# The first blocks of the first attention inside the projections, and two small jobs moved into the attention

## The reference

```
xr, gr, q, k, v = jnp.split(h @ ev_w_in, 5, axis=-1)        # 512 columns each
xr = causal_dwconv(xr, ev_conv_w, ev_conv_b)
hr = rg_lru(xr, ...)            # gates a, u; recurrence h = a * h_prev + u along the tokens
ya = hr * gelu(gr)
q = rms_norm(q per head of 64, ev_qn_g);  k = rms_norm(k per head, ev_kn_g)
yb = stick_breaking(q, k, v)
mix = concatenate([ya, yb]) @ ev_w_out

# stick_breaking, 8 heads, strictly causal mask
z   = q k^T / 8
sp  = where(mask, softplus(z), 0)
rev = reversed cumulative sum of sp over the keys
out = exp(where(mask, z - rev, -inf)) @ v
```

## Time and profile before

| | |
|---|---|
| median of three runs | 3681.15 us |
| the profiled execution | 3685.37 us |
| its span in the trace | 3683.6 us |
| TensorE busy | 3588.1 us (97%) |
| VectorE busy | 1978.4 us (54%) |
| ScalarE busy | 1333.8 us (36%) |
| mean granted TensorE clock | 0.979 of full |
| projections of q and k, attention | about 107 to 163 us, 163 to 250 us |

### The profile page before, as it was taken

How to read it: one execution, slowest core, us unless ns; L and a number is a source line. 1 busy time by engine, 2 the same in 40 slices (tenths; PEclk the granted TensorE clock), 3 DMA queues, 4 the chain that set the end, 5 groups by cost and what they waited for, 6 DMA issues and landing times.

```text
span 3683.6 us, 41651 instructions
## 1 busy us (share of the span) xinstructions
PE 3588.1 (97%) x16738; PEld 2891.5 (78%) x16738; DVE 1978.4 (54%) x3590; ACT 1333.8 (36%) x2316; POOL 31.8 (1%) x40
## 2 busy tenths in 40 slices
PE   7999999999999999998999999999999999989998
PEld 6668888757888888885788888888878888778886
DVE  7766666675756554576774236423643333354233
ACT  4653333453423332334533223323333233343222
POOL 0000000000000000001100000000000000000000
PEclk9999999999999999999999999999999999989999
DMA  7224555303555455521023222222222222112221
GB/s 280 98 103 149 199 194 177 121 35 121 194 194 194 143 194 194 193 102 40 29 72 100 97 97 81 98 97 97 81 90 82 75 84 82 54 61 97 97 97 63
DMA packets 155613, 429.18 MB, mean 117 GB/s; under 512 B 45483, under 2 KB 50667, under 8 KB 155420
## 3 DMA queue, kind: packets, MB, share of 16 engines
q1 hardware_dynamic: 155420, 426.51, 34.2%
HBM read 424.04 MB, written 2.40 MB: 116 GB/s over the span
## 4 chain that ended last, share of the span: by engine, by line
PE 91%; DVE 6%; ACT 2%; issue 1%; DMA 0%; SPq 0%; POOL 0%; ACTq 0%; DVEq 0%; POOLq 0%
PE ps L427 26%; PE ps L429 26%; PE ps L428 26%; PE ps L746 1%; PE ps L726 1%; PE ps L464 1%; PE ps L786 1%; PE ps L824 1%; PE ps L582 1%; PE ps L599 1%; PE ps L811 1%; PE ps L610 1%; PE ps L477 1%; PE ps L734 1%; DVE wlo L1519 0%
## 5 line engine op out<-in xcount | busy, mean ns | idle before, releaser
L427 PE MATMUL ps<-HH,whi 128*128 128x512 f32 x3168 | 1251.8, 395 | 16.7 <-DVE HL L1576 7.1
L429 PE MATMUL ps<-HH,wlo 128*128 128x512 f32 x3168 | 1236.0, 390 | 0.0
L428 PE MATMUL ps<-HL,whi 128*128 128x512 f32 x3168 | 1235.3, 390 | 0.0
L1519 DVE TENSOR_TENSOR wlo<-wraw,whi 128x1024 fp32r<-128x1024 f32 x548 | 670.8, 1225 | 793.4 <-ACT whi L948 793.1
L948 ACT ACTIVATE whi<-wraw 128x1024 fp32r<-128x1024 f32 x548 | 575.4, 1054 | 714.8 <-PE ps L429 705.9
L427 PEld LDWEIGHTS ps<-HH,whi 128*128 128x128 f32 x3168 | 596.4, 188 | 153.7 <-issue 24.0
L428 PEld LDWEIGHTS ps<-HL,whi 128*128 128x128 f32 x3168 | 596.6, 188 | 125.3 <-issue 4.3
L429 PEld LDWEIGHTS ps<-HH,wlo 128*128 128x128 f32 x3168 | 596.0, 188 | 125.9
L1509 DVE CUSTOM_DVE_ANT_0 mraw<-mraw,CB 128x1024 f32<-128x1024 f32 x224 | 273.0, 1219 | 0.6 <-DMA mraw<-mst 0.6
L1710 DVE TENSOR_TENSOR TT<-TT,ps 128x512 f32<-128x512 f32 x116 | 79.7, 687 | 202.0 <-PE ps L429 171.3
L427 PE MATMUL ps<-PHf,whi 128*128 128x512 f32 x352 | 136.9, 389 | 0.0
(11 more groups left out here) (332 smaller groups left out, 3815.3 us busy)
## 6 DMA issues: line engine op xcount, KB each, us to landing
wraw<-wst SPq DMA_DIRECT2D x548, 512.0 KB, 3.3
mraw<-mst SPq DMA_DIRECT2D x224, 512.0 KB, 4.2
MR<-mst SPq DMA_DIRECT2D x16, 512.0 KB, 14.1
X<-xt SPq DMA_DIRECT2D x8, 256.0 KB, 5.8
BB<-bvec SPq DMA_DIRECT2D x8, 256.0 KB, 3.5
TT<-lse SPq DMA_DIRECT2D x16, 128.0 KB, 2.9
out<-X SPq DMA_DIRECT2D x8, 256.0 KB, 2.0
CB<-crow SPq DMA_DIRECT2D x2, 512.0 KB, 4.4
```

The source lines that it names most:

```text
L427: e.matmul(o[key], wh, sh(k), start=k == 0, stop=False)
L428: e.matmul(o[key], wh, sl(k), start=False, stop=False)
L429: ins = e.matmul(o[key], wl, sh(k), start=False, stop=k == nk - 1)
L1519: e.tensor_tensor(wlo[:, b % RAW, :], wraw[:, b % RAW, :], whi[:, b % SPLIT, :].bitcast(F32), ALU.subtract).then_inc(*wlo_made.up(b))
```

## The change

Logits 0 to 5 stand inside projections 5, 6 and 7 (two each), and the running sums of blocks 0 and 1 inside projection 7. Attention begins with the sums of block 2 and step 6. The head norm of projection 7 is issued in step 6, its root on ScalarE in step 6, its scaling on VectorE ahead of step 7. The rings of banks for norms and logits are reordered. The scratch tiles of `logs` are four in turn (2, 0, 3, 4) instead of five; tile 1 is left to the last norm. The scan writes `YA`, which lies where `YL` lies; `lru_high` is issued in steps 8, 11, 14, 17 and `lru_low` in steps 9, 12, 15, 18. The ten `mod_step`s are issued from step 7 on instead of step 4. Functions not shown here are unchanged; `weights_of` moves out of `stick` with its text unchanged.

```
         YL = at("YL", ph + 8192, [P, 4, S], F32R)
+        YA = at("YA", ph + 8192, [P, 4, S])
...
-        st_slot = (2, 3, 4, 2) + (0, 1, 3, 4, 2) * 6
+        st_slot = (2, 3, 4) * 2 + (2, 0, 3, 4) * 7
...
-            ev_norms = Ring(2, 3, 2, 3, 2, 3, 2, 5)
-            zb = Ring(0, 1, 4, 3, 2, 5)
+            ev_norms = Ring(2, 3, 2, 3, 2, 3, 3, 6)
+            zb = Ring(0, 1, 4, 2, 5, 3)
...
# TensorE, even(): heads(i, k)
+                first_heads = ((5, 5), (5, 7), (6, 1), (6, 5), (7, 1), (7, 5))
...
-                    elif (i, k) in ((6, 5), (6, 7), (7, 1), (7, 5)):
-                        logits(2 * (i - 6) + (k > 5 if i == 6 else k > 1))
+                    elif (i, k) in first_heads:
+                        logits(first_heads.index((i, k)))
+                        if i == 7:
+                            later_sums(first_heads.index((i, k)) - 4)
...
# TensorE, stick(); sums(i) is moved out as later_sums(i), text unchanged
-                qk_norm("ev", 7, ev_order[7], ev_norms)
-                for t in range(3, 39):
-                    if 3 < t < 32:
+                later_sums(2)
+                for t in range(6, 39):
+                    if t < 32:
                         logits(t)
+                    if t == 6:
+                        qk_norm("ev", 7, ev_order[7], ev_norms)
                     if t < 35:
-                        sums(t - 3)
+                        later_sums(t - 3)
...
# ScalarE: lru_high reads YA; even()
-                    if i - 1 in lru_steps:
-                        lru_high(lru_steps.index(i - 1))
                     if i in lru_steps:
                         lru_root(lru_steps.index(i))
+                    if i >= 6:
+                        logs(2 * i - 11)
                     if i == 7:
-                        logs(1)
-                        logs(2)
+                        logs(4)
                     if i:
                         qk_rsqrt("ev", i - 1, ev_order[i - 1])
-                        if i == 6:
-                            logs(0)
-                        elif i == 7:
-                            logs(3)
-                    qk_square("ev", i, m, ev_order[i - 2])
+                    if i in (5, 6):
+                        logs(2 * i - 10)
+                    if i < 7:
+                        qk_square("ev", i, m, ev_order[i - 2])
+                    if i == 7:
+                        weights_of(0)
...
# ScalarE: logs(i)
-                if i < 2:
+                if i < 3:
                     lane.wait_ge(v_mix, ("gi", 3))
-                elif i == 2:
-                    lane.wait_ge(v_mix, ("yl", 3))
-                elif i in (4, 5):
-                    lane.wait_ge(v_mix, ("qk", "ev", ev_order[i + 2]))
+                elif i == 7:
+                    lane.wait_ge(v_mix, ("qk", "ev", ev_order[6]))
                 else:
-                    lane.wait_ge(v_mix, ("a1", i - 5 if i > 5 else 0))
+                    lane.wait_ge(v_mix, ("a1", i - 3 if i < 7 else i - 4))
...
# ScalarE: stick()
-                qk_rsqrt("ev", 7, ev_order[7])
-                weights_of(0)
-                for t in range(4, 39):
+                logs(5)
+                weights_of(1)
+                qk_square("ev", 7, ev_order[7], ev_order[5])
+                weights_of(2)
+                for t in range(6, 39):
                     if t < 32:
                         logs(t)
                     if t < 35:
                         weights_of(t - 3)
+                    if t == 6:
+                        qk_rsqrt("ev", 7, ev_order[7])
+                    if t in (8, 11, 14, 17):
+                        lru_high(t // 3 - 2)
...
# VectorE: lru_scan writes YA[:, m, :] instead of T[4] and no longer waits for ("yl", m - 1); lru_low reads YA; even()
-                    if i - 1 in lru_steps:
-                        lru_low(lru_steps.index(i - 1))
...
-                    if i == 7:
-                        softplus(1)
                     if i:
                         ev_norm(i - 1)
-                    if i >= 6:
-                        softplus(2 * i - 12)
+                    if i >= 5:
+                        softplus(2 * i - 10)
+                        softplus(2 * i - 9)
...
# VectorE: stick()
-                softplus(3)
-                ev_norm(7)
-                for t in range(4, 40):
+                for t in range(6, 40):
+                    if t == 7:
+                        ev_norm(7)
                     if t < 32:
                         softplus(t)
-                    if t % 3 == 1 and t < 34:
-                        mod_step(29 + (t - 4) // 3)
+                    if t in (9, 12, 15, 18):
+                        lru_low(t // 3 - 3)
+                    if t % 3 == 1 and t < 36:
+                        mod_step(29 + (t - 7) // 3)
```

More of the change, by code:

```diff
@@ L586, in logits, with later_sums @@
                          stop=True, skip_group_check=True).then_inc(*mm_done.up(("z", h, kt)))
+            def later_sums(i):
+                h, kt = block_of(i)
+                n, o = wid[kt], ps[:, bank_of[("z", h, kt)], :]
+                later, ones = CR["nlater"][:], CR["nones"][:]
+                lane.wait_ge(v_mix, ("spl", i))
+                for k2 in range(kt, 4):
+                    n2 = wid[k2]
+                    for part in (SPH, SPL):
+                        ins = e.matmul(o[:, n - n2:n], later if k2 == kt else ones, part[h % 3][:, off[k2]:off[k2] + n2],
+                                       start=False, stop=k2 == 3 and part is SPL, skip_group_check=True)
+                ins.then_inc(*mm_done.up(("lat", h, kt)))
             def stick():
                 ob = Ring(6, 7)
[L590 to L601, removed]
                 def heads_out(h, kt):
@@ L1135, in lru_high @@
                 lane.wait_ge(v_mix, ("ya", m))
-                e.activation(YH[:, m, :], T[4], ACT.Copy).then_inc(*a_mix.up(("yh", m)))
+                e.activation(YH[:, m, :], YA[:, m, :], ACT.Copy).then_inc(*a_mix.up(("yh", m)))
             def even():
@@ L1200, in logs, with weights_of @@
                 e.activation(l, l, ACT.Ln, bias=1.0).then_inc(*a_mix.up(("log", i)))
-            def stick():
[L1204 to L1211, removed]
-                qk_rsqrt("ev", 7, ev_order[7])
-                weights_of(0)
-                for t in range(4, 39):
+            def weights_of(i):
+                h, kt = block_of(i)
+                n, o = wid[kt], off[kt]
+                lane.wait_ge(mm_done, ("lat", h, kt))
+                if h >= 3:
+                    lane.wait_ge(mm_done, ("so", h - 3))
+                e.activation(SNB[h % 3][:, o:o + n], bank(("z", h, kt))[:, 0:n], ACT.Exp).then_inc(*a_mix.up(("w", h, kt)))
+                freed[("z", h, kt)] = ((a_mix, ("w", h, kt)),)
+            def stick():
+                logs(5)
[3 more added lines that the diff above has]
+                for t in range(6, 39):
                     if t < 32:
@@ L1813, in lru_scan @@
             def lru_scan(m):
-                z, xc = T[4], XC[:, m, :]
+                z, xc = YA[:, m, :], XC[:, m, :]
                 lane.wait_ge(a_mix, ("sqr", m))
@@ L1818, in lru_scan @@
                 lane.wait_ge(a_mix, ("lb", m))
-                if m:
-                    lane.wait_ge(v_mix, ("yl", m - 1))
                 e.tensor_tensor_scan(z, RR[:, m, :], xc, 0.0, ALU.mult, ALU.add).then_inc(*v_mix.up(("scan", m)))
@@ L1825, in lru_low @@
             def lru_low(m):
-                keep_low(YL[:, m, :], T[4], YH[:, m, :], a_mix, ("yh", m), ("yl", m))
+                keep_low(YL[:, m, :], YA[:, m, :], YH[:, m, :], a_mix, ("yh", m), ("yl", m))
             def even():
```

## The result

The changed kernel took 3724.56 us, the median of four executions (3722.94 to 3727.05), beside 3681.03 for the kernel before in the same session: 1.0094 of its time [1.0052, 1.0137]. The forecast was 3677 and its range ended at 3691. The profiled execution took 3724.93 us, of which the span is 3723.1; that is 39.6 us above the profiled execution of before.

The account below looks back on a forecast made before the run. TensorE's queue bounds the kernel, its low clock the largest loss. Waits net 0.9 us gained, plus 4.1 from the clock, less 0.9 for a dip: 4 us off 3681.15, so 3677, range 3667 to 3691.

Parts of the forecast that it names:

- The two late projections: Projections starting at 132.93 and 139.97 us would lose their 0.45 us waits on VectorE: 0.8 to 1.2 us gained.
- The wait at (7, 5): Inside projection 7, logits(5) waits for VectorE's read of norm 6 to free bank 3: 1.5 us, range 1.3 to 2.5.
- a dip of the clock: Short clock dip at the 1.5 us wait inside projection 7: up to 1.7 us, half likely, 0.9 taken.
- The wait at the first weighted-value matmul: At step 7, heads_out waits for the last norm's read to free bank 6: 1.9 us, range 1.0 to 2.3.
- nothing ahead of it can shorten this: For the step 7 wait: ScalarE stands at the sums, so no work ahead of it can reduce the 1.9 us.
- No other wait in steps 8 to 31: In attention, TensorE doesn't wait on ScalarE or VectorE; moved splits and four T slots cost zero.
- The fall of the clock at 172.6 to 176: TensorE's clock falls to its low level near the first weighted-value matmul, after the 1.9 us wait.
- If the clock is back at the same place of the order as now: Clock returns between the end of step 10 and step 11's logits: 4 us gained in all, chance 0.48.
- price of 0.45 us for each us of it: Time lost per us at TensorE's low clock, from the same attention steps timed at both levels; 10.7 us before the change.
- The rival "stays low longer": Low clock in attention lasts one head longer, 3.7 us slower (0.10), or two or more, from 11.4 slower (0.14).
- the Trainium skill's two readings weighed in the prediction: For TensorE's waits: the low clock belongs to an idle engine, or short idle spells between matmul groups make the clock swing.

Follow-up runs that it names:

- the kernel with the norm alone: Kernel before with only the last head norm moved to step 6, bank 6, root after block 3's weights, four scratch tiles: 3722.35 us, ratio 1.0052.
- the kernel with the splits alone: Kernel before with only the recurrence's rounding and subtraction moved into attention steps 8 to 18, the scan writing YA: 3717.11 us, ratio 1.0011.
- the kernel before shifted by 0.5 us: Kernel before with six unread matmuls ahead of projection 5, making all that follows later: 3687.18 us, ratio 1.0004.

## Why the prediction was wrong

**The two late projections, 1.2 us gained: right.** No wait is left there, and each projection takes 6.43 to 6.51 us, 6.46 forecast.

**The wait at (7, 5), 1.5 us: right**, 1.44, with a dip of the clock of 3.4 us behind it that had been given one chance in two (there in the first two profiles, not in the third). No row gave its price, up to 1.7; with the dip the norm matmuls of attention and of the last projection stand 9.96 us apart, without it 8.37, so it cost 1.6.

**The wait at the first weighted-value matmul, 1.9 us: right**, 1.78, released by the norm's read as forecast. ScalarE's weights of block 3 ahead of the root were a named term (0.58 us); moving the root ahead of them shortened the wait by 1.1. The prediction's "nothing ahead of it can shorten this" was a misreading. In the changed kernel ScalarE waits 0.52 us for block 3's running sums, which the root doesn't need, and then runs the weights:

```profile
171.75 0.60 ACT L1213 ACTIVATE SNB<-ps 128x512 f32<-128x512 f32 x1 [0.52 <-PE ps L601]
172.25 0.68 ACT L1096 ACTIVATE RS<-ps,EPSC 128x512 f32<-128x512 f32 x1
```

**No other wait in steps 8 to 31: right.** The splits and the four T slots are hidden.

**The fall of the clock at 172.6 to 176: right**, at 174.7 (173.9 and 175.4 in the other two profiles).

**"If the clock is back at the same place of the order as now": the step that failed.** In the first execution it wasn't: 109.2 us at the low level instead of about 15. At the prediction's own price of 0.45 us for each us of it that is 49 us against 10.7 before, 38 more, where 39.1 were measured. I had read the end of the low stretch from one profile of one execution, as if it belonged to the order of the work. It does not. It was back in the first head in the second and third profiles of the changed kernel (189.0 and 187.6), and not until the last head in the first, with the same waits. The rival "stays low longer" had the mechanism, but its price stopped at two heads (11.4 us), and its chance at 0.14. The profiles show why two is not a natural limit. In all whose clock fell there it rose either within 24 us or only where the attention ends (105.8 to 109.2 us later). The heads repeat, at 17.2 us each and with the same work. That what doesn't raise the clock in one head doesn't in the next either is my reading of this; no run tests it.

**The result was a draw, and a loaded one.** The first four executions were all long, the four of before all short; over all executions it is 15 of 28 against 22 of 117. So the size of the first ratio is partly luck of the draw. That the change makes long executions more frequent rests on the counts, which one session of the three doesn't bear out, and on the kernel with the norm alone (10 of 12). That it is the waits through which the clock falls is shown by the kernels that shorten or fill them: 0 long in 66 executions, of the changed kernel, of its parts and of before, and in none of their six profiles does the clock fall within the first attention. Of the Trainium skill's two readings weighed in the prediction, these runs side with the one on short idle spells (same page, section "A second HAM failure mode: psum-queue depth-cycling").

**Open.** What sets the share of long executions where the clock does fall: the kernel with the splits alone has the waits of before to a hundredth and 7 long of 12, and the kernel before shifted by 0.5 us had 1 of 12. But these are two sessions, and the unchanged kernel before had 10 of 29 in the one and 2 of 30 in the other. So something that differs from session to session (they ran on different chips) may have a part in it, and no run here separates it from the place of the attention against the fall. The waits' lengths alone don't explain it: with the same 1.78 us in all its three profiles the changed kernel did both.

## What to carry to other kernels

A wait in thin work can be priced by what the clock does after it, up to the end of the repeated work, and not by its own length: here 1.8 us of waiting cost up to 50. So read from the profile how long the low level could last at worst, take several executions before you trust where it ended, and compare counts, not only medians. Shortening such a wait by moving one instruction on another engine, or filling it with matmuls nobody reads, left no long execution in 66.

## What was not expected of the hardware

TensorE kept to its low level for 109.2 us with hardly any idle time in the profile, and nothing in the instructions forbids the high one: the same program ran them at 1.00 over 200 to 220 in its two other profiles. Two executions of one program on the same inputs differed by up to 63 us (3666.21 and 3729.66). Of this the first attention gives 45 in the profiles (244.38 and 289.31); the rest lies behind it, where the odd attention had 34.1 us at the low level in the first profile and 20.4 in the third. The times between 3706 and 3715 were empty in all kernels.
